# Hybrid decoder layer in float32 on one core: the order of SP's slab loads, of VectorE's quarter sums, and of the columns of x

## What is computed

```python
z = u @ w_in[l]
c_q, c_kv, k_r, rq, rk, rv, rg, gates = jnp.split(z, cuts, axis=-1)
g_a, g_r = jnp.split(jax.nn.sigmoid(gates + b_gate[l]), 2, axis=-1)
h = h + (g_a * y_a + g_r * y_r) @ w_out[l]
```

## Time and profile before

| | us |
|---|---|
| median of 3 runs | 1842.6 (1841.13 to 1847.04) |
| the profiled execution, its own time | 1846.3 |
| its span, first to last instruction | 1844.5 |
| PE busy in the span | 1758.1 (95%) |
| DVE busy | 1169.2 (63%) |
| POOL busy | 958.6 (52%) |
| ACT busy | 734.5 (40%) |
| mean granted TensorE clock | 0.981 of full speed |

### The profile page before, as it was taken

How to read it: one execution, slowest core, us unless ns; L and a number is a source line. 1 busy time by engine, 2 the same in 40 slices (tenths; PEclk the granted TensorE clock), 3 DMA queues, 4 the chain that set the end, 5 groups by cost and what they waited for, 6 DMA issues and landing times.

```text
span 1844.5 us, 25039 instructions
## 1 busy us (share of the span) xinstructions
PE 1758.1 (95%) x8527; PEld 1463.9 (79%) x8527; DVE 1169.2 (63%) x1637; ACT 734.5 (40%) x1307; POOL 958.6 (52%) x564
## 2 busy tenths in 40 slices
PE   7999999998689889998999999999999999999998
PEld 7888888886567777787878888778888888888887
DVE  5655663645354887876244554778777777789852
ACT  6422223342122666732122332554544444444432
POOL 6743333334256577654443224377777777666540
PEclk9999999998889999999999999999999999999999
DMA  6511111334564688673221124234334343485322
GB/s 262 204 46 40 40 34 58 114 130 145 199 229 149 227 317 309 233 253 136 81 92 58 58 69 169 89 97 136 121 111 140 107 137 119 159 303 182 120 80 92
DMA packets 119634, 260.30 MB, mean 141 GB/s; under 512 B 7936, under 2 KB 58752, under 8 KB 115072
## 3 DMA queue, kind: packets, MB, share of 16 engines
q1 hardware_dynamic: 84656, 180.03, 28.9%
q10 hardware_dynamic: 34896, 79.18, 11.8%
HBM read 184.73 MB, written 73.92 MB: 140 GB/s over the span
## 4 chain that ended last, share of the span: by engine, by line
PE 75%; DVE 9%; ACT 5%; DMA 4%; issue 3%; POOL 3%; ACTq 1%; SPq 0%; DVEq 0%; POOLq 0%
PE ps L840 12%; PE ps L845 12%; PE ps L846 12%; PE ps L1509 7%; PE ps L1514 7%; PE ps L1511 7%; PE ps L1584 3%; PE ps L1586 3%; PE ps L1585 3%; DMA raw<-in_slabs 2%; ACT prow L2063 2%; POOL wl L738 2%; PE ps L1260 1%; PE ps L1280 1%; DVE aneg L2952 1%
## 5 line engine op out<-in xcount | busy, mean ns | idle before, releaser
L723 POOL TENSOR_SCALAR wh<-raw 128x1024 fp32r<-128x1024 f32 x59 | 168.1, 2849 | 417.7 <-PE ps L840 381.5
L1633 ACT ACTIVATE wh<-raw 128x512 fp32r<-128x512 f32 (+1 forms) x200 | 127.9, 650 | 161.8 <-PE ps L1514 58.0
L772 POOL TENSOR_TENSOR wl<-raw,wh 128x512 fp32r<-128x512 f32 x88 | 136.4, 1560 | 73.2 <-ACT wh L1633 71.9
L840 PE MATMUL ps<-uh,wh 128*128 128x512 f32 x368 | 147.2, 400 | 7.4 <-POOL wl L725 6.7
L759 POOL TENSOR_TENSOR over_rings<-over_rings 128x512 f32<-128x512 f32 x92 | 118.2, 1286 | 52.2 <-DMA over_rings<-in_slabs 46.8
L725 POOL TENSOR_TENSOR wl<-raw,wh 128x1024 fp32r<-128x1024 f32 x59 | 142.7, 2418 | 4.9
L846 PE MATMUL ps<-uh,wl 128*128 128x512 f32 x368 | 144.6, 393 | 0.0
L845 PE MATMUL ps<-ul,wh 128*128 128x512 f32 x368 | 144.3, 392 | 0.0
L815 POOL TENSOR_TENSOR wl<-raw,wh 128x512 fp32r<-128x512 f32 x63 | 94.5, 1510 | 73.8 <-ACT wh L1633 73.8
L2487 DVE SCALAR_TENSOR_TENSOR ya<-zA,sm,ya 128x512 f32<-128x512 f32 x88 | 109.3, 1242 | 32.7 <-ACT ya L2311 25.5
L738 POOL TENSOR_TENSOR wl<-raw,wh 128x512 fp32r<-128x512 f32 x36 | 52.0, 1456 | 108.9 <-ACT wh L1633 108.9
(11 more groups left out here) (529 smaller groups left out, 5314.5 us busy)
## 6 DMA issues: line engine op xcount, KB each, us to landing
raw<-in_slabs SPq DMA_DIRECT2D x106, 512.0 KB, 3.6
over_rings<-in_slabs SPq DMA_DIRECT2D x22, 1024.0 KB, 7.4
s_s<-over_rings SPq DMA_DIRECT2D x22, 1024.0 KB, 4.9
ssm<-s_s SPq DMA_DIRECT2D x22, 512.0 KB, 4.5
raw<-s_s SPq DMA_DIRECT2D x22, 512.0 KB, 3.8
s_f<-yb ACTq DMA_DIRECT2D x22, 512.0 KB, 5.3
raw<-s_d SPq DMA_DIRECT2D x36, 256.0 KB, 2.5
raw<-in_slabs SPq DMA_DIRECT2D x27, 256.0 KB, 4.6
```

The lines of the kernel that those rows point to most:

```text
L723: pool.tensor_scalar(wh[:, j, :], raw[:, j % RAWS, :], 1.0, None, ALU.mult).then_inc(S["w_hi"], 1)
L772: pool.tensor_tensor(wl[:, v // 2, half(v % 2)], src, wh[:, v // 2, half(v % 2)].bitcast(f32), ALU.subtract).then_inc(S["v_ready"], 1)
L840: l = pe.matmul(o, lh, rh, start=start, stop=False, skip_group_check=onto)
```

## The change

Three things are reordered; no arithmetic is added or taken away.

1. In SP's order the two raw slabs of a pair are issued ahead of the store and the load of the down sums, and so are the latent slabs, two and two.
2. In DVE's order of a pair the quarter u4 stands ahead of the weight sums VS1, VS3 and VS2 of the next pair, not between them.
3. The columns of x come in two groups of CH = 4 with a semaphore each (the second, `xc_ld`, is the semaphore `par` counted on). ACT issues four ahead of its first split, and one after each of steps 0 to 3. TensorE waits for the first group ahead of block 0 and for the second ahead of block 4.

```diff
+        S["xc_ld"], XC0 = S["par"], 48 + 32 * (GP - 2)
...
             for i in range(GP):
-                if i >= 2:
-                    if i > 2:
-                        down_store(i - 3)
-                    down_load(i - 2)
                 for r in range(RAWS):
                     gate_slab(i, r)
+                if i > 2:
+                    down_store(i - 3)
+                if i >= 2:
+                    down_load(i - 2)
             for n in range(2):
+                slab(SLAB0["lat"] + 2 * n)
+                slab(SLAB0["lat"] + 2 * n + 1)
                 down_store(GP - 3 + n)
                 down_load(GP - 2 + n)
-                slab(SLAB0["lat"] + 2 * n)
-                slab(SLAB0["lat"] + 2 * n + 1)
...
-            pe.wait_ge(S["x_ld0"], 16 + 16 * KB)
+            pe.wait_ge(S["x_ld0"], 16 + 16 * CH)
...
             for m in range(1, KB):
+                if m == CH:
+                    pe.wait_ge(S["xc_ld"], XC0 + 16 * CH)
...
-                              x[:, m * P:(m + 1) * P].rearrange("(t p) n -> p t n", p=P)).then_inc(S["x_ld0"], 16)
-            for m in range(2):
+                              x[:, m * P:(m + 1) * P].rearrange("(t p) n -> p t n", p=P)).then_inc(
+                    S["x_ld0" if m < CH else "xc_ld"], 16)
+            for m in range(CH):
                 residual_in(m)
...
-                if m + 2 < KB:
-                    residual_in(m + 2)
+                if m < CH:
+                    residual_in(CH + m)
...
                     gate_times(i - 1, "B0")
+                quarter(i, "u4")
                 if more:
                     gate_sum(i + 1, VS1)
                     gate_sum(i + 1, VS3)
-                quarter(i, "u4")
-                if more:
                     gate_sum(i + 1, VS2)
                 quarter(i, "c22")
```

More of the change, by code:

```diff
@@ L496, in build @@
         ZST0 = {"zA0": 16 * (GD // 2 + KB // 2), "zA1": 16 * (GD // 2 + KB // 2), "zB0": 16, "zB1": 16}
-        d_done, d_free = (S["done0"], S["done1"]), (S["free0"], S["free1"])
         def gz_store(name, i):
@@ L515, in g_gate @@
             return z[:, half(b)]
+        d_done, d_free = (S["done0"], S["done1"]), (S["free0"], S["free1"])
         LANDED = {(name, c): (S[n], at + 16) for name, c, n, at in (
@@ L3439, in _ @@
                 onto(c21, 6, m, ALU.add)
-            dve.wait_ge(S["x_ld0"], 16 + 16 * KB + 16)
+            dve.wait_ge(S["x_ld0"], 16 + 16 * CH + 16)
             for n in range(NT):
```

## The result

| | before | after |
|---|---|---|
| median, us | 1841.9 (1840.9 to 1847.0) | 1811.8 (1810.3 to 1814.4) |
| the profiled execution, us | 1846.3 | 1813.2 |
| its span, us | 1844.5 | 1811.4 |
| granted TensorE clock | 0.981 | 0.991 |

The ratio is 0.9833, with a 95% interval of 0.9809 to 0.9856: 30 us faster, where 42 were forecast. 1811.8 lies just above the range (1792 to 1811). The parts for the gate pairs and the latent slabs have the forecast sign. The part for x, forecast as a gain of 1.6 us, is a loss.

The account below looks back on a forecast made before the run. TensorE, 95% of the span, was taken as the bound, through its waits. Gains of 33.5 (pairs), 6.9 (latent slabs) and 1.6 (x) sum to 42.0 us: 1842.6 to 1800.6, say 1801; range 1792 to 1811.

Parts of the forecast that it names:

- Edit 1, the pairs: Gate pairs 2 to 4: slabs issued ahead of store and load, with u4 moved, remove the whole 33.5 us.
- the 2.3 us to spare in pair 4: Gate pair 4: u4 ends at 11.3 us after the pair's start, wanted by TensorE at 13.6.
- DVE's loop of 20.2 us: Gate pairs: DVE's work per pair takes 20.2 us against TensorE's 19.04, so u4's end slips 1.2 us a pair.
- Edit 2: DVE's order in the gate pairs: u4 ahead of the sums gives 4.7 us of cover, untouched by a late slab.
- rival C: Slab issues held by POOL and stay put; only u4's move acts, 24.6 us remain: gain 10.5, 1832; chance 0.03.
- Edit 1, the latent slabs: First latent slab gains 9.65 us, the second gets a new 2.8 us wait: net 6.9, bounds 2.0 and 9.7.
- The new wait: Second latent slab: TensorE waits 2.8 us for bank 0, held until the gates' last store has landed.
- Edit 3: Block 0 of w_out: 5.91 us wait for x goes, longer ACT hold costs some back; gain 1.6, bounds -2.4 and 3.2.
- The sign that was to show it: At x: no wait for the DMA, but TensorE waits of L845 for DVE's `mil`.
- Rival B: Issues of x don't hold ACT, so x gains 8.7 us in place of 1.6: 1793.5; chance 0.12.
- Rival A: DMA becomes the limit of the gate pairs, leaving 8 to 10 us of waits: 1809 to 1811; chance 0.15.
- D: Gate pairs: later down-sum loads make DVE and then TensorE wait; slower than before, 1849 at 16 us excess; chance 0.02.

Follow-up runs that it names:

- the late issues with two groups: Kernel after, but no column of x issued ahead of ACT's first split of the mix, two groups kept: 1798.83 us, ratio 0.9772 to the kernel before.

## Why the prediction was right, and where it failed

Of the 42.0 us forecast 28.4 came at the change's places: the pairs gave 2.0 less than forecast, the latent slabs 6.4 less, x 5.2 less.

**Edit 1, the pairs: right, but with none of the room that was worked out.** 33.5 forecast, 31.5 found. The slabs no longer wait for the load, and the down rows were there when DVE asked (landed at 444.95, asked for at 448.90). But the second slab of pair 2 was issued at s+5.7 and landed at s+11.0, where s+3.6 and s+7.6 were forecast, and the store took 6.6 us to land for 3.9. u4 ended at s+10.4, 12.5 and 13.6 in pairs 2, 3 and 4, forecast 8.9, 10.1 and 11.3: the 2.3 us to spare in pair 4 were not there. Pairs 2 and 3 took 19.04 us each, pairs 4 and 5 20.01 and 20.24: DVE's loop of 20.2 us that the prediction worked out does become the bound, and it reaches TensorE first at another place than u4 or c22, at which I had laid its slack. Timelines of DVE (c21 of pair 3, behind the down sums), of ACT and of TensorE (the fifth product of pair 4), after:

```profile
472.88 0.68 DVE L2796 TENSOR_TENSOR gzB<-gu,ps 128x512 f32<-128x512 f32 x1
```

```profile
473.59 0.72 ACT L1873 ACTIVATE gzB<-gzB,sm 128x512 f32<-128x512 f32 x1 [5.09 <-DVE gzB L2796]
...
474.22 0.58 ACT L1636 ACTIVATE gu<-ps 128x512 f32<-128x512 f32 x1
```

```profile
474.85 0.50 PE L1057 MATMUL ps<-uh,wh 128*128 128x512 f32 x1 [0.67 <-ACT gu L1636]
```

c21 hands its sum to ACT's sigmoid, ACT's copy of the first product's bank stands behind that sigmoid, and TensorE's fifth product needs that bank. It waits 0.67 us here and 0.90 in pair 5, and the two pairs together are 2.2 us over 2 x 19.04. I had counted the loop's slip at two of its customers and called it covered; this third one, with the least cover, was left out.

**Edit 2: no error in the sum, one in its weight.** It was priced as the keeper of 4.7 us of cover. It is hardly needed: with edit 1 alone the median is the same, and u4 holds TensorE for 2.1 us in all. The working of rival C (24.6 us stay with late slabs) was wrong by the loop: all 33.5 stay.

**Edit 1, the latent slabs: mis-sized.** The gain at the first slab, 9.65 forecast, was 9.4. The new wait was named with its place and its chain (last product, store, bank 0, the second slab), but at 2.8 us, bounds 0 and 7.6; it took 5.7, and the lower clock behind it 3.2 more. Two terms of it failed. The last product was stretched either way (2.77 before, 2.83 after), but it starts 3.1 us later against TensorE's first latent product (4.25 us behind 535.57 before, 7.32 behind 503.39 after). Some 2.2 of that are the product of gzA, beside which POOL's residue of a latent slab now falls: 2.83 us after, and before

```profile
534.37 0.69 DVE L2801 TENSOR_TENSOR gzA<-gzA,gyA 128x512 f32<-128x512 f32 x1 [0.79 <-ACT gzA L1870]
```

The other 0.8 is DVE's own lag behind TensorE from the pairs. And I took the wait without the lower clock that followed each of the long waits of before. With both, 2.8 + 3.1 + 2.8 = 8.7, against 8.9 measured. The Trainium skill (SBUF — State Buffer, section "SBUF: two separate sides") gave the better sign: by the shared lock the wait was to be near the upper bound, my estimate from it was some 5 us, and it was 5.7. The rows of POOL agree only in part, and they decide: the stretch came with POOL's residue in all eight profiled executions in which the last product fell beside one; POOL's high part, which reads SBUF too, left it at 0.69 in five and at 1.29 in one.

**Edit 3: the step of the mechanism that failed.** The shift of ACT's first split was forecast at 4.8 to 8.3 us; against the end of the mix it is 4.8. The failure is one step on: "TensorE now needs four columns of x in place of eight: its wait of 5.91 us before 846.07 goes", with a start at 840.2. That row has one releaser, the last to come, and behind it stood a second wait, bank 0, that the multiply of the mix's last step frees. Row of the timeline of DVE before:

```profile
844.72 0.68 DVE L3023 TENSOR_TENSOR sab<-ps,sab 128x512 f32<-128x512 f32 x1
```

It ends at 845.40, 0.7 us ahead of 846.07. So at most 0.7 of the 5.91 could go, and the shift of 4.8, which I had let play out at the thirteenth residue, acts here in full: 0.7 - 4.8 = -4.1. Block 0 starts 4.2 us later against the mix, and -3.6 is left at its end. The sign that was to show it, waits for the residues `mil`, did not come for this reason. Rival B (8.7 us gained without a longer hold) fell for the same reason: with two columns ahead and two groups 1.2 us came, within the scatter. That the hold is real was shown by the late issues with two groups, 9.6 us.

**Sum.** With these terms 31.5 + 0.5 - 3.6 = 28.4, against 30.1 of the medians. Rival A (DMA the limit of the pairs, 1809 to 1811) gave the nearest time, by a way that the trace doesn't show: the pairs hold 19.04 us where DVE lets them. What rivals C and D describe is not in the trace either: the slabs' issue did move, and DVE didn't wait for the down rows.

What stays open is why the store behind a stretched product also lands later (DVE's next entry came 4.4 to 4.8 us after it in the eight profiled executions with a stretched one, 3.4 in four without).

## What to carry to other kernels

A wait of TensorE that a load ends tells nothing of the other waits in front of the same instruction: before a wait is booked as a gain, look for every semaphore that the instruction needs and for when each came, and book only the distance to the next. A step taken out of a loop gains nothing unless it is the one that closes the loop. DMAs issued on a computing engine's queue behind many others can hold that engine, here for 7 to 15 us; issued some steps later, and in two groups so that the consumer needs only half of them at first, they cost it nearly nothing.

## What the runs showed of the hardware

- Two issues of 512 KB columns held ACT's queue for 7.1 to 8.8 us, four for 14.1 to 15.1, at the start of the mix behind twelve other loads; in the kernels with late issues, from the mix's third step on, an issue took 0.39 to 0.72.
- The last gate product, a DVE TENSOR_TENSOR of 128x512 with both inputs in SBUF, took 2.77 to 2.83 us beside POOL's residue (TENSOR_TENSOR, 2.3 to 2.4 us; eight executions) and 0.69 (five) or 1.29 (one) beside POOL's high part (TENSOR_SCALAR, 2.8 to 3.3 us). Over the whole trace of before, of 39 such operations of DVE that started inside a high part and touched no other operation of POOL's, 28 took 0.7 us and the longest 1.52; of 120 that started inside a TENSOR_TENSOR of POOL's the median is 1.77 and the longest 2.92.
- At the second latent slab a TensorE that had stood still for 1.50 or 1.69 us went on with matmuls at the full clock; after 1.97 us, in another kernel's execution at the same place, it went on at 1.2 GHz (the first matmul 0.76 us, then one each 0.43) for 3.5 us, and after 5.6 to 5.8 us, in five executions, for 3 to 6 us.
